# Layer 1 gates and branch products with tokens on partitions, merged units turned back by TensorE

## The reference

```python
h = rmsnorm(x, norm_attn[l])
(..., q_h, f_h, i_h, g_h, gates) = jnp.split(h @ w_in[l], split_at, axis=-1)   # gates: 3 x 2048 columns
o_nsa = nsa_mixer(...); o_sb = stick_breaking(...); o_hg = hgrn2(q_h, f_h, i_h, g_h, ...)   # 1024 wide each
branches = jnp.stack([o_nsa, o_sb, o_hg], axis=2)
y = jnp.einsum('btnc,ncd->btnd', branches, w_branch[l])
gsig = jax.nn.sigmoid(gates).reshape(B, T, N_BRANCH, D_MODEL)
merged = jnp.sum(gsig * y, axis=2)
x = x + merged @ w_out[l]
```

## Time and profile before

| | |
|---|---|
| median of 3 runs | 2743.68 us (2743.63 to 2744.79) |
| profiled execution | 2743.38 us, span 2741.6 us, mean granted TensorE clock 0.999 |
| PE busy | 2722.4 us (99%) |
| PE weight loads busy | 2361.9 us (86%) |
| DVE busy | 1875.9 us (68%) |
| ACT busy | 1268.5 us (46%) |
| POOL busy | 63.4 us (2%) |
| DMA | 544.12 MB, mean 198 GB/s |

### The profile page before, as it was taken

One profiled execution on the slowest core, in us unless ns is written; L12 is line 12 of the kernel. 1 busy time (PEld: TensorE's weight loads), 2 busy tenths in 40 slices (PEclk: granted clock), 3 DMA queues, 4 the chain that ended last, 5 costly groups with the idle time before them and its releaser, 6 DMA issues.

```text
span 2741.6 us, 37778 instructions
## 1 busy us (share of the span) xinstructions
PE 2722.4 (99%) x14992; PEld 2361.9 (86%) x14992; DVE 1875.9 (68%) x2085; ACT 1268.5 (46%) x1214; POOL 63.4 (2%) x113
## 2 busy tenths in 40 slices
PE   9999999999999999999999999999999999999998
PEld 8888888888888888888888888888888888888887
DVE  8675656777667879877777455665555756665686
ACT  6455457634645535544444333433333345453542
POOL 0000000000000000000000000000000000000100
PEclk9999999999999999999999999999999999999999
DMA  7765444555456555555555655555555466557853
GB/s 274 231 228 167 158 159 164 182 204 194 160 217 239 210 198 208 184 186 194 186 185 193 222 199 184 202 185 197 185 193 179 169 208 213 192 192 241 310 208 138
DMA packets 129439, 544.12 MB, mean 198 GB/s; under 512 B 10893, under 2 KB 17038, under 8 KB 82224
## 3 DMA queue, kind: packets, MB, share of 16 engines
q1 hardware_dynamic: 120096, 510.95, 53.1%
q0 software_dynamic: 9232, 31.57, 3.3%
HBM read 523.50 MB, written 23.04 MB: 199 GB/s over the span
## 4 chain that ended last, share of the span: by engine, by line
PE 92%; DVE 4%; ACT 2%; DMA 1%; issue 0%; SPq 0%; DVEq 0%; ACTq 0%
PE gemm L703 31%; PE gemm L706 16%; PE mix L703 6%; PE gemm L760 4%; PE gemm L762 4%; PE gemm L761 4%; PE mix L1079 4%; PE mix L706 3%; PE mix L1077 2%; PE mix L760 2%; PE mix L762 2%; PE mix L761 2%; DVE wlo L1783 1%; DMA raw<-wstream 1%; PE gemm L1079 1%; PE mix L1242 1%
## 5 line engine op out<-in xcount | busy, mean ns | idle before, releaser
L1275 ACT ACTIVATE whi<-raw 128x2048 fp32r<-128x2048 f32 x466 | 891.3, 1913 | 1172.5 <-DMA raw<-wstream 1169.8
L1783 DVE TENSOR_TENSOR wlo<-raw,whi 128x2048 fp32r<-128x2048 f32 x465 | 1064.7, 2290 | 479.4 <-ACT whi L1275 478.3
L703 PE MATMUL gemm<-HX,whi 128*128 128x512 f32 x3840 | 932.4, 392 | 1.9 <-DVE scratch L1808 0.7
L703 PEld LDWEIGHTS gemm<-HX,whi 128*128 128x128 f32 x3840 | 705.2, 188 | 139.3 <-issue 2.8
L706 PEld LDWEIGHTS gemm<-HX,wlo 128*128 128x128 f32 x3840 | 493.1, 191 | 17.5
L706 PE MATMUL gemm<-HX,wlo 128*128 128x256 f32 x3840 | 498.9, 283 | 0.0
L760 PE MATMUL gemm<-whi,HX 128*128 128x512 f32 x512 | 202.6, 396 | 1.2 <-DVE arena L1955 1.2
L762 PE MATMUL gemm<-wlo,HX 128*128 128x512 f32 x512 | 199.6, 390 | 0.0
L761 PE MATMUL gemm<-whi,HX 128*128 128x512 f32 x512 | 199.2, 389 | 0.0
L1808 DVE TENSOR_REDUCE arena<-gemm 128x256 f32<-128x512 f32 (+1 forms) x97 | 66.9, 689 | 142.3 <-PE gemm L703 142.2
L1079 PE MATMUL mix<-ACTX,whi 128*128 (+1 forms) x528 | 138.5, 392 | 0.3
(11 more groups left out here) (438 smaller groups left out, 2766.9 us busy)
## 6 DMA issues: line engine op xcount, KB each, us to landing
raw<-wstream SPq DMA_DIRECT2D x462, 1024.0 KB, 4.8
scratch<-gate_scratch POOLq DMA_DIRECT2D x12, 512.0 KB, 4.9
raw<-wstream SPq DMA_DIRECT2D x10, 512.0 KB, 5.5
gate_scratch<-scratch SPq DMA_DIRECT2D x32, 128.0 KB, 4.6
GL<-gate_scratch POOLq DMA_DIRECT2D x8, 512.0 KB, 5.0
gate_scratch<-arena SPq DMA_DIRECT2D x16, 256.0 KB, 6.2
gate_scratch<-gates_vc SPq DMA_DIRECT2D x16, 256.0 KB, 6.3
bias_scratch<-row_scratch POOLq DMA_DIRECT2D x21, 192.0 KB, 5.2
```

Of the source, the lines that this page charges most:

```text
L703: return pe.matmul(bank.rearrange("p (c t) -> p c t", c=2), whi[slot][:, w(k)], mx(k), start=k == 0, stop=k == total - 1)
L1275: f(whi[slot][:, :], raw[slot][:, :], ACT.Copy).then_inc(s["hi_ready"], 1)
L1783: tt(wlo[slot][:, :], raw[slot][:, :], whi[slot][:, :].bitcast(F32), ALU.subtract).then_inc(s["lo_ready"], 1)
```

## The change

Layer 1's gates become twelve groups of four blocks, in the form that layer 2's have. Their bank pairs follow the table in `pair_of_group` (0 is `gemm0`, `gemm1`; 2 is `mix[2:4]`; 4 is `mix[4:6]`), and `bank_free` says for whose evacuation PE waits. Each group is evacuated by two copies after its fourth block. A new semaphore `hg_dd` holds the third group until DVE has read the diagonal sums from `mix[2:4]`. `hg_o` comes one block later than before. The branch products become units: two blocks give 512 columns for 256 tokens in one bank pair of `mix[0:4]`, and one DVE product of 128 x 1024 with the gate follows. For the third branch PE turns each merged unit back (`turn1`, into `mix[4:6]`), ACT and DVE split it from there. The line numbers below are those of the changed kernel.

```diff
-V_GROUPS += tuple(range(B_G2, B_Y2, 4))
+V_GROUPS += tuple(range(B_G, B_Y, 4)) + tuple(range(B_G2, B_Y2, 4))
+Y_GROUPS = tuple(range(B_Y, B_O, 4))
+N_U = 4
...
+        def pair_of_group(g):
+
+            if B_G <= g < B_Y:
+                return (0, 0, 2, 0, 2, 0, 2, 0, 2, 0, 4, 0)[(g - B_G) // 4]
+            return 4 * ((g - B_G2) // 4 % 2) if B_G2 <= g < B_Y2 else 0
+
+        def bank_free(g, t):
+
+            first = B_G if g < B_Y else B_G2
+            before = [h for h in range(first, g, 4) if pair_of_group(h) == pair_of_group(g)]
+            if not before:
+                return None if pair_of_group(g) else use(g) + t - 1
+            return use(before[-1]) + t + 1
+
+        def gate_blocks(g):
+
+            k = (g - B_G) // 4
+            first = B_G + 16 * (k // 4) + 8 * (k % 4 // 2) + k % 2
+            return slice(first, first + 8, 2) if B_G <= g < B_Y else slice(g, g + 4)
+
+        def unit_tiles(view, u):
+
+            return view[:, 8 * (u // 2) + u % 2:8 * (u // 2) + 8:2, :]
...
+                if b == 0 and g == B_G + 8:
+                    pe.wait_ge(s["hg_dd"], 1)
...
+                    if b == 0 and bank_free(g, t):
+                        pe.wait_ge(s["evac_done"], bank_free(g, t))
+                    bank = gate_bank(g, t).rearrange("p (c f) -> p c f", c=4)
...
+            def unit_block(ps, n, k0, total, xh, xl):
+
+                slot = n % RING
+                wh = whi[slot][:, :].rearrange("p (c k f) -> p k c f", c=4, k=4)
+                wl = wlo[slot][:, :].rearrange("p (c k f) -> p k c f", c=4, k=4)
+                for t in range(2):
+                    bank = ps[t].rearrange("p (c f) -> p c f", c=4)
+                    for k in range(4):
+                        h, l = xh(k0 + k, cols(t)), xl(k0 + k, cols(t))
+                        pe.matmul(bank, h, wh[:, k], start=k0 + k == 0, stop=False)
+                        pe.matmul(bank, l, wh[:, k], start=False, stop=False)
+                        ins = pe.matmul(bank, h, wl[:, k], start=False, stop=k0 + k == total - 1)
+                ins.then_inc(s["gemm_done"], 1)
...
+            def merged_turn(sem, done, free, mg, u, banks):
+
+                pe.wait_ge(sem, done)
+                if free:
+                    pe.wait_ge(s["mg_l"], free)
+                for t in range(2):
+                    for c in range(4):
+                        o, to = u * 1024 + t * 512 + c * P, (c % 2) * T + t * P
+                        ins = turn(banks[c // 2][:, to:to + P], mg[:, o:o + P])
+                ins.then_inc(s["mg_t"], 1)
+
+            def turn1(u):
+
+                merged_turn(s["y1_sum"], N_U + u + 1, u, MG1, u, [M[:, 4 + c, :] for c in range(2)])
+
...
+            def branch(b):
+
+                x = OX[b % 2]
+                for i in range(N_Y):
+                    n, u, h = B_Y + b * N_Y + i, i // 2, i % 2
+                    unit = N_U * b + u
                     pe.wait_ge(s["lo_ready"], n + 1)
-                    pe.wait_ge(s["evac_done"], u0 + i - 1)
-                    for c in range(2):
-                        ins = group(y_banks(u0 + j)[:, c, :], range(8), 8, lambda k: cols(c * 8 + k), lambda k: x[:, k, :],
-                                    lambda k: x[:, k::8, :], slot)
-                    ins.then_inc(s["gemm_done"], 1)
-                blocks(pe, n0, N_Y, body)
-
-            def pair(n0, sem, marks, mh, mx, between=None, free=None, after={}):
+                    if h == 0 and unit >= 2:
+                        pe.wait_ge(s["y1_out"], unit - 1)
+                    unit_block([M[:, 2 * (u % 2) + t, :] for t in range(2)], n, 4 * h, 8, lambda k, w: x[:, k, w],
+                               lambda k, w: x[:, 8 + k, w])
+                    if b == 2 and h == 0 and u:
+                        turn1(u - 1)
+
...
-            advance(1)
+            advance(2)
             pe.wait_ge(s["hg_a"], 8)
             pe.wait_ge(s["hg_cc"], 1)
+            pe.wait_ge(s["evac_done"], use(B_G0) + 2)
...
             ins.then_inc(s["hg_o"], 1)
-            advance(3)
+            advance(2)
             pe.wait_ge(s["head_sq"], 3)
...
-                branch(B_Y + n * N_Y, OX[n % 2])
-            pair(B_O, s["mg_l"], [(5, 10), (N_Y, KT)], hk, xk, free=use(B_Y))
+                branch(n)
+            pair(B_O, s["mg_l"], [(2, 8), (N_U, KT)], hk, xk, after=(8, lambda: turn1(3)))
...
+            def to_scratch(n, bank, i, j, it):
+
+                g = group_of(n)
+                if n == g + 3:
+                    act.wait_ge(s["evac_done"], use(g) + 2)
+                    c = (g - B_G0) // 4
+                    f(SCR[:, c * 1024:(c + 1) * 1024], SCR[:, c * 1024:(c + 1) * 1024], ACT.Sigmoid).then_inc(s["g0_sig"], 1)
...
+            def unit_high(u):
+
+                act.wait_ge(s["mg_t"], u + 1)
+                f(unit_tiles(HH, u), M[:, 4:6, :].rearrange("p b (a t) -> p (b a) t", a=2), ACT.Copy).then_inc(s["mg_h"], 1)
...
+                if i % 2 and i > 2:
+                    unit_high(i // 2 - 1)
+                plain(B_Y + 2 * N_Y + i, 1)
+            unit_high(3)
...
                         return
                     dve.wait_ge(s["gemm_done"], n + 1)
                     for t in range(2):
...
+                            d = gring[layer][t]
+                            if k:
+                                dve.wait_ge((gate1_out, gate2_out)[layer][t], 16 * k)
+                        dve.tensor_copy(d, gate_bank(g, t)).then_inc(s["evac_done"], 1)
...
-                    me.link(ins)
+                    ins.then_inc(s["hg_dd"], 1)
+                    dve.wait_ge(s["hg_dd"], 1)
...
+            def gated1(b, u):
+
+                unit, c = N_U * b + u, slice(u * 1024, (u + 1) * 1024)
+                if b:
+                    dve.wait_ge(s["g_sig"], unit - N_U + 1)
+                dve.wait_ge(s["gemm_done"], B_Y + b * N_Y + 2 * u + 2)
+                y = M[:, 2 * (u % 2):2 * (u % 2) + 2, :].rearrange("p a b -> p (a b)")
+                product(y, s["y1_out"], s["y1_sum"], unit, b == 0, (SCR, GL, SCR)[b][:, c], MG1[:, c], tmp1[u % 2])
+
+            def unit_low(u):
+
+                dve.wait_ge(s["mg_h"], u + 1)
+                tt(unit_tiles(HL, u), M[:, 4:6, :].rearrange("p b (a t) -> p (b a) t", a=2), unit_tiles(HH, u).bitcast(F32), ALU.subtract
+                   ).then_inc(s["mg_l"], 1)
...
+            for b in range(3):
+                for i in range(N_Y):
+                    if i % 2:
+                        if b == 2 and i > 2:
+                            unit_low(i // 2 - 1)
+                        gated1(b, i // 2)
+                    plain(B_Y + b * N_Y + i, 1)
+                    if b == 1 and i == 3:
+                        operand(2)
+            unit_low(3)
```

More of the change, by code:

```diff
@@ L110, in plain_end @@
 def plain_end(n, end):
-    return min([g for g in V_GROUPS if g > n] + [end])
+    return min([g for g in V_GROUPS + Y_GROUPS if g > n] + [end])
 def use(n):
@@ L320, in build @@
  hg_ln hg_k hg_kq hg_kl hg_d xv hg_x0 hg_x1 hg_x2 hg_s hg_a hg_c hg_cc
- hg_o hg_ge hg_out
- o_h o_l y_second g_sig y_done y2_out y2_sum mg_t mg_h mg_l x_back x_saved
+ hg_dd hg_o hg_ge hg_out
+ o_h o_l y1_out y1_sum g_sig y2_out y2_sum mg_t mg_h mg_l x_back x_saved
  c_id f_exp f_act f_hi f_lo dn_tile xd_done x2_saved x2_back
@@ L555, in _ @@
             reloads(B_WOVEN + len(WOVEN) + 1, B_G)
-            blocks(sp, B_G, 2 * N_G, spill)
-            reloads(B_G0, B_G2)
+            for n in range(B_G, B_G0 + 1):
+                reload(n, n % RING, n // RING, 0, 0)
+                if n > B_G and (n - B_G) % 4 == 0:
+                    spill(0, (n - B_G) // 4 - 1)
+            reloads(B_G0 + 1, B_G2)
             for n in range(B_G2, B_Y2 + 1):
@@ L614, in _ @@
                 bias(h, h)
-            for r in range(4):
-                pool.wait_ge(gate_out[r], 8 * 16)
+            for t in range(2):
+                pool.wait_ge(gate1_out[t], 8 * 16)
             for k in range(4):
@@ L623, in _ @@
                 if k == 0:
-                    pool.wait_ge(s["evac_done"], use(B_Y + N_Y))
+                    pool.wait_ge(s["y1_out"], N_U)
                 gates_back(1, SCR[:, :], k)
@@ L762, in values @@
                         ins = pe.matmul(bank, xh, wl[:, k], start=False, stop=kk == KT - 1)
[L763 removed]
+                    if b == 3 and t == 0 and g in V_GROUPS[:N_VALUES]:
                         ins.then_inc(s["v_half"], 1)
                 ins.then_inc(s["gemm_done"], 1)
[L767 to L779 removed]
@@ L785, in pair @@
+            def pair(n0, sem, marks, mh, mx, between=None, after=None):
                 u0, k0 = use(n0), 0
-                pe.wait_ge(s["evac_done"], free or u0 - 1)
+                pe.wait_ge(s["evac_done"], u0 - 1)
                 for count, k1 in marks:
@@ L797, in pair @@
                             norm_sums(between[0])
-                    if k1 in after:
-                        merged_turn(after[k1])
+                    if after and after[0] == k1:
```

(29 more changed lines are left out.)

196 lines of the change are left out of this document (47 added, 149 removed).

## The result

The changed kernel takes 2753.92 us in the median of 6 runs (2751.73 to 2756.56), the kernel before 2744.08 in 6 runs beside them (2743.20 to 2745.20). The ratio is 1.0036, 95% interval 1.0026 to 1.0047: slower by 9.8 us, where 2750.0 was forecast with a range from 2742.5 to 2753.5; the median lies 0.4 us outside it. The profiled execution took 2751.73, with a span of 2749.7: 8.1 us more than before, where the sum had 6.3. So the sum missed by 1.8 us, and the median lies 2.2 us above the profiled execution, not 0.3.

A forecast was written before the change was run, and what follows sets the result against it. PE, busy 99% of the span, bounds the kernel. Costs of 15.2 us against gains of 10.4 make 4.8 longer, 6.3 with the clock: 2749.7 profiled, 2750.0 median, 8 in 10 range 2742.5 to 2753.5.

The forecast's parts named there:

- Pace: Layer 1 gate blocks and branch blocks on PE drop to 5.44 us, gaining 5.6 and 3.3 us.
- two removed waits: PE's waits at its fourth gate block (0.9 us) and at the sums behind `hg_o` (0.6 us) go.
- The group switch: PE's fifth gate block waits 5.9 us for the first group's first copy, behind DVE's level 0 operands.
- The sums behind `hg_o`: With two blocks there instead of three, PE waits 3.3 us for DVE's low half of the squares.
- The turns: Third branch: four turns of eight PE transposes, 0.79 us each, cost 3.4 us in all.
- the last turn: Ahead of the second half of `pair`, PE waits 2.6 us for the last unit's split by ACT and DVE.
- The clock: PE's clock falls to half 4.3 us into a wait, so only at the 5.9 us wait; costs 1.5 us.
- rival 4: The clock falls at every wait and stays low long: 2758, intermediate cases from 2753; chance 0.08.
- Rival 1: All waits come but the clock holds: 2748.5; chance 0.28.
- rival 2: The group switch costs nothing, as DVE gets to the copies by 520.0: 2742.6; chance 0.11.
- rival 3: All three waits are hidden and only the turns cost: 2736.7; chance 0.06.
- Rival 5: PE's pace goes by columns alone, so the 8.9 us gain does not come: 2758.9; chance 0.02.

The follow-up runs named there:

- bank: Changed kernel with the first gate group in mix[4:6] instead of gemm0 and gemm1, DVE's order kept; 2744.41 us, ratio 1.0001.
- mid: Changed kernel with DVE evacuating the first gate group directly behind the first of four level 0 operations instead of behind all four; 2748.72 us.
- all three: Changed kernel with the edits of bank, sums and evens together; 2736.98 us, ratio 0.9973 to the kernel before.
- first profile: Profiled execution of the changed kernel, no further edit, among the six runs of the result; 2751.73 us.
- second profile: Profiled execution of the changed kernel when run again with no edit; 2755.52 us, where the median of those 5 runs was 2753.34.
- sums: Changed kernel with PE taking the sums of the squares three blocks behind `hg_o` instead of two; 2748.43 us, ratio 1.0014.
- evens: Changed kernel with PE doing k tiles 8, 10, 12, 14 of both blocks behind the last turn, then the odd ones; 2749.67 us, ratio 1.0020.
- fillers: Changed kernel with 24, 12 and 10 extra PE products into unused banks during the three waits; 2749.06 us, ratio 1.0018.

## Why the prediction was wrong, step by step

**Pace, right.** Blocks of 5.44 us instead of 5.56 and 5.58, at both places. With the waits out of the way the gates' stage is 7.1 us shorter, the forecast's 5.6 for the pace and 1.5 for the two removed waits.

**The group switch, right.** 5.96 us against 5.9. The bank and mid kernels show both of its conditions: without the shared bank pair it goes, and moving the copies by three operations shortens it by 3.5 us.

**The sums behind `hg_o`, right in mechanism, 2.9 against 3.3.** PE came to them at 741.0, 11.1 us behind the restart at 729.91 where 10.9 was said, and the low half of the squares began at 741.58, 11.7 behind it, where the forecast's chain gives 11.9.

**The turns and the last turn, right.** 0.79 us a turn and 2.4 us against 2.6. That the turns are hidden in nothing is shown by what is left in the kernel with all three edits: 0.8 us gained in the branches out of 3.3.

**The clock, wrong.** This is the failed step. The forecast took one row, a fall 4.3 us after PE's last product, as a delay that a wait must exceed ("The wait of 5.9 us is longer, the others (3.3 and 2.6) are shorter"), and charged 1.5 us once. The runs show in its place:

- The delay is not fixed. After PE's stop at the first group the clock fell after 2.9 us (first profile), 4.3 (second), 5.4 (sums), 4.6 (evens) and 2.6 (mid); at the sums behind `hg_o` after 2.0 to 2.5, where it fell; behind the last turn after 2.0 to 3.5. Three of these falls came when PE had already gone on, by 0.2 us (mid), 0.3 (sums, last turn) and 1.2 (second profile, last turn).
- Even the row that was read is one of several values. At the program's end, in the nine profiles, the clock falls 1.2 to 4.3 us after PE's last product, and the 4.3 of the kernel before is the longest. The shortest is in the second profile, where PE's last products end at 2742.94 and a window with 0.60 was at half level for 0.8 us:

```profile
2741.93 1.01 PE L1287 MATMUL mix<-vc,ones_r 128*128 128x128 f32 x4 [0.26 <-DVE vc L2597]
2744.00:2745.00 1.00, 0.00 (x0) 0.00 (x0) 0.96 (x3) 0.00 (x0) 0.00 (x0) 0.60 0.00 0
```

- All waits of 2.4 us and more are candidates. In the six profiles that have such waits with PE idle in them, the place of the first wait drew a fall 5 times out of 5, the last turn 5 out of 5, the sums 3 out of 5.
- A stretch is 3.4 or 6.8 us long, and only its part behind PE's restart costs, half of it: 1.5 to 3.1 us each. A count without that halving agrees. From the restart to the third group PE takes 27.27, 27.90, 28.40, 28.01 and 27.13 us in the five profiles with the first wait, in the order above, and 25.43 in the two without it (bank, all three): 1.7 to 3.0 us more. Together the falls cost 3.5 us in one profile and 7.2 in the next.

So the term was worth 3.5 us in the profiled execution where 1.5 stood, 7.2 in the next profile and, by the fillers, 4.3 in the median. The forecast set the median 0.3 above the profiled execution as in the kernel before, which has no such waits. The profiled execution was the shortest of its six, 2.2 below their median; in the five runs that followed, the profiled one lies 2.2 above. Where it falls among the runs is chance, and no single profile of such a kernel gives its median. The mean clock of the six runs goes with their time: 0.997 in the three up to 2753.44, 0.996 and 0.995 in the three from 2754.40.

The rest of the sum, 4.8 us without the clock, held: the two profiles are 8.1 - 3.5 = 4.6 and 12.0 - 7.2 = 4.8 above the kernel before, and the fillers' kernel, which has all waits and no fall, lies 5.3 above it in the median. In part this is luck. The waits came to 11.2 us instead of 11.8 and the turns to 3.2 instead of 3.4, and the 0.5 outside the change makes up for most of that.

**The rivals.** What happened is between the forecast and rival 4 (2758, "with intermediate cases from 2753"). It got 0.08, and "two waits are below 4.3 us" was the reason; that reason was the error. Rival 1 (2748.5) is the fillers' kernel (2749.1), rival 2 (2742.6) the bank kernel (2744.4, with two falls left), rival 3 (2736.7) the kernel with all three edits (2737.0). As none of them is the changed kernel itself, they fell as forecasts but the prices held. Rival 5 falls with the pace: both forms have 12,288 columns in a block, and the one takes 5.44 us, the other 5.56.

**What stays open.** Why the sums' wait of 2.9 us draws no fall in two profiles of five, while waits of 2.4 us drew one each time, and why a fall can come 2.0 or 5.4 us after PE's stop: the trace gives the moment of a fall, not its rule. The fillers gave back 4.3 us in the median where 5.5 were expected, and the difference was not traced. And the 0.9 us by which the first gate block is later than in the one profile of the kernel before were not traced; nothing that the change touches lies ahead of it.
